# Moving the turn of the attention weights, its values product and the head means to one border between weight units

## The reference

```
h = rms_norm(x); p = h @ w_in                   # 32 column blocks of 128
A (4 heads): softmax(q1 k1) - lam * softmax(q2 k2), times v, rms_norm over the head
             q, k: rms_norm over 64, rotary; heads of 128 columns
B (4 heads): gated linear recurrence forward and backward, rms_norm, * silu(g)
x = x + concat(A, B) @ w_out
x = x + conv_glu(rms_norm(x))                   # up 1024 -> 5632, conv width 3, down 2816 -> 1024
```

## Time and profile before

| | |
|---|---|
| time, median of 3 runs | 1427.21 us (1421.37 to 1427.74) |
| profiled execution | 1427.63 us, span 1425.8 us |
| PE busy | 1396.5 us, 98% |
| PEld (weight loads, beside PE) | 1127.1 us, 79% |
| DVE / ACT / POOL busy | 845.6 / 615.7 / 704.7 us |
| mean granted PE clock | 0.994 of 2.4 GHz |
| first 40 slots | about 0 to 330 us in layer 0, about 730 to 1040 us in layer 1 |

### The profile page before, as it was taken

One profiled execution on the slowest core, in us unless ns is written; L12 is line 12 of the kernel. 1 busy time (PEld: TensorE's weight loads), 2 busy tenths in 40 slices (PEclk: granted clock), 3 DMA queues, 4 the chain that ended last, 5 costly groups with the idle time before them and its releaser, 6 DMA issues.

```text
span 1425.8 us, 18800 instructions
## 1 busy us (share of the span) xinstructions
PE 1396.5 (98%) x6562; PEld 1127.1 (79%) x6562; DVE 845.6 (59%) x1096; ACT 615.7 (43%) x881; POOL 704.7 (49%) x539
## 2 busy tenths in 40 slices
PE   8999999999999999999989999999999999999999
PEld 6877877877788888888868778777777888888887
DVE  7755798455667766600347767975557776675001
ACT  6343555474444444412443335554644444443211
POOL 2675376237344444444556953753374444444443
PEclk9999999999999999999999999999999999999999
DMA  5222122122223232333222231121232333233323
GB/s 182 73 68 85 54 63 75 45 60 89 89 89 101 93 102 89 95 101 102 88 74 74 67 92 53 57 74 45 62 102 74 103 93 100 89 100 94 101 91 115
DMA packets 37124, 121.31 MB, mean 85 GB/s; under 512 B 4928, under 2 KB 5440, under 8 KB 37056
## 3 DMA queue, kind: packets, MB, share of 16 engines
q1 hardware_dynamic: 36768, 119.84, 27.0%
q10 hardware_dynamic: 288, 0.52, 0.1%
HBM read 114.05 MB, written 2.10 MB: 81 GB/s over the span
## 4 chain that ended last, share of the span: by engine, by line
PE 80%; POOL 5%; issue 5%; DVE 5%; ACT 3%; DMA 0%; POOLq 0%; DVEq 0%; ACTq 0%
PE bank L536 23%; PE bank L538 22%; PE bank L537 22%; PE bank L615 3%; POOL wL L476 2%; PE bank L673 2%; PE bank L691 2%; PE bank L578 2%; POOL rstd L390 1%; POOL wL L470 1%; PE bank L682 1%; DVE hL L378 1%; PE bank L646 1%; ACT wH L856 1%; PE bank L571 1%
## 5 line engine op out<-in xcount | busy, mean ns | idle before, releaser
L476 POOL TENSOR_TENSOR wL<-raw,wH 128x1024 fp32r<-128x1024 f32 x142 | 342.2, 2410 | 420.7 <-ACT wH L864 358.3
L536 PE MATMUL bank<-hH,wH 128*128 128x512 f32 x1216 | 489.0, 402 | 17.6 <-DVE T L1244 7.4
L538 PE MATMUL bank<-hL,wH 128*128 128x512 f32 x1216 | 476.9, 392 | 0.0
L537 PE MATMUL bank<-hH,wL 128*128 128x512 f32 x1216 | 476.6, 392 | 0.0
L470 POOL TENSOR_TENSOR wL<-raw,wH 128x256 fp32r<-128x256 f32 x268 | 244.1, 940 | 197.8 <-ACT wH L856 197.8
L536 PEld LDWEIGHTS bank<-hH,wH 128*128 128x128 f32 x1216 | 230.0, 189 | 90.1 <-issue 20.6
L538 PEld LDWEIGHTS bank<-hL,wH 128*128 128x128 f32 x1216 | 229.8, 189 | 50.1
L537 PEld LDWEIGHTS bank<-hH,wL 128*128 128x128 f32 x1216 | 230.2, 189 | 44.6 <-issue 0.5
L864 ACT ACTIVATE wH<-raw 128x1024 fp32r<-128x1024 f32 x116 | 122.5, 1056 | 184.4 <-PE bank L538 184.4
L856 ACT ACTIVATE wH<-raw 128x1024 fp32r<-128x1024 f32 x93 | 98.3, 1057 | 138.0 <-PE bank L538 137.9
L536 PE MATMUL bank<-gH,wH 128*128 (+1 forms) x352 | 137.3, 390 | 0.0
(11 more groups left out here) (164 smaller groups left out, 1746.0 us busy)
## 6 DMA issues: line engine op xcount, KB each, us to landing
raw<-wts SPq DMA_DIRECT2D x210, 512.0 KB, 3.5
x<-xT SPq DMA_DIRECT2D x8, 256.0 KB, 5.4
swp<-K SPq DMA_DIRECT2D x32, 64.0 KB, 2.0
swp<-QO SPq DMA_DIRECT2D x32, 64.0 KB, 2.6
outT<-x SPq DMA_DIRECT2D x8, 256.0 KB, 2.0
raw<-wts ACTq DMA_DIRECT2D x2, 256.0 KB, 4.7
raw<-wts SPq DMA_DIRECT2D x2, 256.0 KB, 5.5
W<-pos SPq DMA_DIRECT2D x1, 256.0 KB, 4.6
```

The costliest lines, as they stand in the source:

```text
L476: pool.tensor_tensor(wL[:, s, :], raw[:, s, :], wH[:, s, :].bitcast(F32), ALU.subtract)\
L536: pe.matmul(out, wH[:, s, a:a + P], rhs_h, start=first, stop=False)
L537: pe.matmul(out, wL[:, s, a:a + P], rhs_h, start=False, stop=False)
L538: return pe.matmul(out, wH[:, s, a:a + P], rhs_l, start=False, stop=last)
```

## The change

The turn, the values product and the stat of a step all move to the start of a slot, one slot on. PE's order becomes: **turn(s-19)**, item, scores, **values(s-19)**, **stat(s-1)**, first half of the unit, (stat if s is 34), **tokens** (always here), gather, second half, second carry. ACT's becomes: `high_now(s + 1)`, **back(s-19)**, `fin` of slot s - 1, `head_out`, `stat_square(s)`, gates, slot 12's tables, `high_out`, item, **tokens**, exponentials, silus. `bank6_uses` follows. The code writes step s - 19 as `step_of(s - 2)`. DVE, POOL and SP are as they were.

```diff
--- before.py
+++ after.py
@@ bank6_uses @@
     for s in range(SLOTS):
+        if step_of(s - 2) is not None:
+            uses.append(("turn", step_of(s - 2)))
+        if s - 1 in STATS and s - 1 != LATE:
+            uses.append(("stat", STATS[s - 1]))
         if tokens_of(s) is not None:
             uses.append(("tokens", tokens_of(s)))
         if s == LATE:
-            uses.append(("stat", STATS[s]))
-        if step_of(s - 1) is not None:
-            uses.append(("turn", step_of(s - 1)))
-        if s in STATS and s != LATE:
             uses.append(("stat", STATS[s]))
@@ tensor @@
                     for s in range(SLOTS):
-                        if item_of(s) is not None:
-                            item(item_of(s))
+                        n, done = item_of(s), step_of(s - 2)
+                        if done is not None:
+                            turn(done)
+                        if n is not None:
+                            item(n)
                         if step_of(s) is not None:
                             scores(step_of(s))
-                        late = step_of(s - 1) is None
-                        if tokens_of(s) is not None and not late:
-                            to_tokens(tokens_of(s))
+                        if done is not None:
+                            values(done)
+                        if s - 1 in STATS and s - 1 != LATE:
+                            stat(STATS[s - 1])
                         columns_of = unit_half if s < N_IN else out_half
                         if l or s > 1:
                             columns_of(s, 0)
                         if s == LATE:
                             stat(STATS[s])
-                        if tokens_of(s) is not None and late:
+                        if tokens_of(s) is not None:
                             to_tokens(tokens_of(s))
-                        n = item_of(s)
                         if n is not None and n % PAIR_ITEMS == OUT:
                             gather(n // PAIR_ITEMS)
-                        if step_of(s - 1) is not None:
-                            turn(step_of(s - 1))
                         if l or s > 1:
                             columns_of(s, 1)
-                        if s in STATS and s != LATE:
-                            stat(STATS[s])
                         if n is not None and n % PAIR_ITEMS == CARRY:
                             carry(n // PAIR_ITEMS, 1)
-                        if step_of(s - 1) is not None:
-                            values(step_of(s - 1))
@@ scalar @@
+                        if step_of(s - 2) is not None:
+                            back(step_of(s - 2))
                         if s - 1 in STATS and s - 1 != LATE:
                             fin(STATS[s - 1])
...
-                        if tokens_of(s) is not None:
-                            tokens(tokens_of(s))
                         if s == 12:
...
                         if item_of(s) is not None:
                             item(item_of(s))
-                        if step_of(s - 1) is not None:
-                            back(step_of(s - 1))
+                        if tokens_of(s) is not None:
+                            tokens(tokens_of(s))
                         if step_of(s) is not None:
                             exponentials(step_of(s))
```

## The result

The changed kernel takes 1436.63 us, median of 4 runs (1433.92 to 1437.11), the kernel before 1425.08 (1421.37 to 1427.74): ratio 1.008, 95% interval 1.006 to 1.0099. The forecast was 1439, range 1432 to 1444, slower. The slowdown is under 1% and clear of noise. A later set of runs (experiment 10) gave 1434.91 against 1424.69, ratio 1.0085 (1.0058 to 1.0112). The profiled execution took 1437.11 us with a span of 1435.3, against 1427.63 and 1425.8: 9.5 us more span. Lines of code after the PE part are three lower in the changed kernel (`wT` is L964, was L967).

What follows compares the result with a forecast made beforehand. The prediction took PE as the bound, with 80% of the chain that ended last. Its terms summed as 1427.6 - 8.7 + 15.3 + 5.1 = 1439.3, forecast 1439 us, range 1432 to 1444.

Steps and rivals of the forecast that it cites:

- Slots 32 and 33, ACT late from its tables: End of each layer's step slots: values waits for ACT, late from exponentials, silus and table loads; +3.12 and +2.47 us.
- Slots 31 and 34: Slots without an item to cover ACT's back: values waits until 1.86 us after the border; +0.18 and +1.86 us a layer.
- The semaphore and queue estimate of 1.86: Earliest start of values after the border, behind ACT's high copy, back and about 0.06 us for the semaphore: 1.86 us.
- the end of the stage: Slots 31 to 34 together, at full clock: 7.6 us added a layer, 15.3 in both.
- Slot 13: PE's idle ahead of item(6) and the slow matmuls after it go: 4.5 us gained in layer 0, 0.35 in layer 1.
- Slot 15: PE's wait for POOL's wL goes because grow comes earlier: 0.64 us gained in each layer.
- Slot 18: This slot loses a turn: 0.36 us gained a layer.
- The cuts: Units no longer cut by the turn in slots 19, 21, 22, 25, 26, 29: 0.15 us each, 0.90 gained a layer.
- The clock: PE's clock drops behind the long waits of slots 32 and 33: 2.55 us lost a layer, 5.1 in both.
- the forecast's terms: Both layers: 8.7 us gained ahead of slot 31, 15.3 added in slots 31 to 34, 5.1 lost to the clock.

Runs made afterwards that it cites:

- experiment 10: The changed kernel run again unaltered, in the same set as other experiments: 1434.91 us, ratio 1.0085 to the kernel before.
- Experiment 6: Changed kernel with a plain copy in place of the silu and no table loads around it: 1424.05 us, ratio 0.9996 to the kernel before.
- Experiment 2: Kernel before with one edit, ACT copies the tokens behind its item: 1421.58 us, ratio 0.998.
- second profile: Profiled execution of the unaltered changed kernel in experiment 10: 1432.45 us, span 1430.7.
- experiments 4: Kernel before with ACT's tokens behind its item and stat behind item and scores, turn and values in mid unit: 1428.52 us, ratio 1.0034.
- Experiments 3 to 5: Kernel before with stat behind item and scores, 1433.61 us; plus ACT's tokens behind its item, 1428.52; plus PE's tokens in mid unit, 1428.33.

## Why the prediction was right

*Slots 32 and 33, ACT late from its tables.* The forecast for slot 32 was +3.12 at full clock. Layer 1 had full clock there: 1004.99 to 1017.21 is 12.22 against 8.95, +3.27. The wait was 3.21 (forecast 3.3), the high copy 3.26 behind the border (forecast 3.2). Experiment 6 shows the cause, and that the chain through stat and fin alone isn't one. Slot 33 of layer 1 took 12.78 against 8.57, +4.2: 1.6 of it is the clock, and 2.6 stands against 2.47 forecast.

*Slots 31 and 34.* The forecast was 0.18 and 1.86, and they cost +0.20 (6.26 less 6.06) and +1.85, with 0.11 more in the unit behind. The semaphore and queue estimate of 1.86 from border to values was 1.85 in the trace (278.07 to 279.92, 314.01 to 315.86).

At full clock the end of the stage costs 8.0 us a layer (layer 1: 9.6 less 1.6), where 7.6 was forecast.

*Slot 13.* The forecast was 4.5 in layer 0, and 4.7 was measured (the next border is 4.85 earlier, 0.14 of it already there in slot 12). Experiment 2 shows it comes from the order of ACT alone. *Slot 15.* The forecast was 0.64, the idle shown, and 0.84 was measured: the tag counts from a modelled end that lies 0.2 behind. *Slot 18* gave 0.48 (a lead of 5.69 at its border, 6.17 at slot 19's), where 0.36 was forecast.

*The cuts.* This is the one term that was wrong: 0.90 a layer was forecast and about 0.1 measured between slots 19 and 30 (the lead over the kernel before is 6.17 us at slot 19's border, 146.57 against 152.74, and 6.26 at slot 31's). Counting only the unit was the mistake. A unit is 0.15 shorter uncut, but the turn at the border costs 0.07 more, and values takes 0.99 with stat behind it where it took 0.89 (187.24 to 188.13). That is 1.6 us less gain than forecast. The gains came to 8.4 all the same, against 8.7, since slots 13, 15 and 18 gave more: two misses that nearly cancel.

*The clock.* The forecast was 5.1 us behind the long waits, net of what a slow unit takes off the next wait. In layer 0 of the profile PE lost 2.9 + 1.6, and the wait of slot 33 was 1.15 shorter (2.06 for 3.21), so 3.4 net; in layer 1 it lost 1.6. Together that is 5.0. In the second profile slot 32 took 13.85 us in both layers, 1.6 over the 12.22 at full clock, and slot 33's wait was 0.80 and 0.28 shorter: 2.1 net. So the first profile has the forecast's size and the second less than half of it, and the picture was too tidy: I had it fall four times, and it fell at two or three of the four places, different ones in two executions.

*The balance*, of the two profiled spans: layer 0 -6.3 and +11.4, layer 1 -2.2 and +9.6, together +12.5, where the forecast's terms give -8.7 + 15.3 + 5.1 = +11.7. The span grew 9.5. The 3.0 between are clock again, at a place that the change doesn't touch: an idle of 1.86 us for POOL's `wL` early in the up phase, in both layers. In the profile of the kernel before the clock fell behind it, in that of the changed one it didn't. Windows of the kernel before, then of the changed kernel:

```profile
377.00:381.00 4.00, 4.00 (x12) 3.15 (x11) 2.31 (x5) 2.08 (x3) 1.37 (x1) 0.57 0.46 135
1087.00:1091.00 4.00, 4.00 (x12) 3.11 (x11) 2.32 (x5) 2.09 (x3) 1.36 (x1) 0.58 0.39 131
```

```profile
381.00:385.00 4.00, 3.30 (x14) 2.74 (x15) 2.85 (x5) 1.58 (x2) 0.88 (x2) 1.00 0.41 131
1097.00:1101.00 4.00, 3.34 (x15) 2.75 (x16) 2.86 (x5) 1.58 (x2) 0.88 (x2) 1.00 0.41 131
```

Whether that is chance or a consequence of when PE arrives there isn't settled: of the other kernels' profiles some have the drop in one layer, some in the other, some in both, and those of experiments 4 and 10 in neither. The medians are 10.2 and 11.6 us apart (of 4 runs of the changed kernel in each set), between 9.5 and 12.5, so they don't decide how much of these 3 us belongs to the change. The forecast named neither this place nor its clock. That 1439 is so near the 1437.11 of the profile has some luck in it: with the clock low at this place in both kernels the same terms would have come to about 1440, still in the range.

*What the prediction missed without harm* is bank 6. It walked the engines' queues and found no price for moving tokens to mid unit but the cut. Experiments 3 to 5 show that stat with tokens right behind it costs 1.1 us a slot, and tokens with turn right behind it a wait of 0.7, and that the change as a whole happens to keep them apart. Turn and stat side by side were not tried.

## What to carry to other kernels

When work is moved to a border, ask of every slot what still stands between producer and consumer; the steady slots can be free while the first and last, where the covering work has run out, pay for all. Look there for what another engine does only once, such as a change of activation table. And a matmul bank that several pieces of work share in turn is a queue of its own. Here the second of two users side by side waited 0.7 to 0.9 us for ACT to read the first, though ACT is busy only 43% of the span (of the kernel before).

## What the runs showed that I had not expected

The granted clock does not follow from the length of the idle before it alone. In slot 32 of layer 1 of the changed kernel, behind the same wait of 3.21 us, it held in the first profile and fell in the second. Behind the idle of some 1.85 us in the up phase it fell in the profile of the kernel before and held in both profiles of the changed kernel. Each fall behind the waits for `wT` gave up 1.7 or 3.4 us of clock and cost PE 1.6 or 2.9. The spans of the two profiles of the changed kernel differ by 4.6 us (1435.3 and 1430.7), and 2.9 of them (5.0 less 2.1) are these falls. So terms of that size are to be summed from waits at full clock first.

Second, a half clock ahead of another engine's late copy costs less than it shows: in slot 33 of layer 0 the wait was 2.06 where layer 1 waited 3.21, because slot 32's slowed unit had used up 1.15 us of it.
